# Order of the TensorE work in the dense expert loop: second table's product of block b-1 ahead of the first table's product of block b

## The chip, the core and the metric

One NeuronCore of a Trainium2 chip runs the whole program; the other seven cores are idle. The metric is device time of one execution in microseconds (us), lower is better; each time given is the median of several executions of the same compiled program. Engines are named as in the profile: PE is TensorE (matrix products), DVE is VectorE, ACT is ScalarE, POOL is GpSimd, SP is the engine that issues most plain DMA transfers.

## The reference

One step of a two-layer decoder on 576 tokens (512 of a prompt, 64 of samples). Each layer has a mixer and then an expert part, and the change lies in the expert part, which is run once per layer. It is this function (cut):

```
def peer_ffn(x, w_q, sub_keys, u, v):
    ...
    def block_fn(xb):
        q = (xb @ w_q).reshape(blk, PEER_HEADS, 2, PEER_HALF)
        s = jnp.einsum('thcd,hcnd->thcn', q, sub_keys).astype(jnp.float32)
        s_top, i_top = lax.top_k(s, PEER_TOPK)
        ...
        best_s, best_pos = lax.top_k(cand_s, PEER_TOPK)
        expert = jnp.take_along_axis(cand_e, best_pos, axis=-1)
        gate = jax.nn.softmax(best_s, axis=-1)
        act = jax.nn.gelu(jnp.einsum('td,thkd->thk', xb, u[expert]).astype(jnp.float32), approximate=False)
        return jnp.einsum('thk,thkd->td', (gate * act).astype(xb.dtype), v[expert])
```

There are 16384 experts per layer; expert e has a row u[e] and a row v[e] of 1024 floats (4 KB each). Every token picks 8 heads x 16 experts. Its result is the sum over the picked experts of gate x gelu(x . u[e]) x v[e].

## The kernel before

`peer_hybrid` (line 548) computes this sum in two ways side by side.

**Sparse part**: 256 prompt tokens and the 64 sample tokens get their rows by gather. There are 320 sets (`NSET`); for each set POOL issues one indirect DMA that fetches 128 rows of u into one of six slots `ug` (line 617), and, 20 sets later (`LAG`), one that fetches 128 rows of v into one of six slots `vg` (line 624). Each gather moves 512 KB. DVE does a dot product on each u set (`dot`, line 725) and adds each v set, weighted, to the accumulator (`add_row`, line 743). A slot is fetched again only when DVE is through with it. One pair of `dot` and `add_row` is a step; there are 340 steps.

**Dense part**: for the other 256 prompt tokens all experts are computed, in 128 blocks of 128 experts. For block b:

- SP loads 128 rows of each table, `du` (line 633) and `dv` (line 638), 512 KB each, each in two buffers.
- PE turns the u rows (`turn_rows`, line 839, into `pt`), and ACT copies them into `uT` (line 782).
- PE computes the first product, `hidden(b)` (line 863): rows of u times tokens, into one of two `hid` buffers; ACT applies gelu into one of two `gl` buffers (line 802).
- DVE multiplies by the gates (`product(b)`, line 713).
- PE computes the second product, `output(b)` (line 872): it adds the gated values times the v rows to `out`, which stays in PSUM for all 128 blocks.

In the trace every float32 matmul of the program stands as two records: `hidden` as 16, `output` as 8.

The two parts meet on DVE, whose order is written out: `product(b)`, then the two or three steps that `steps_of(b)` gives to block b (340 steps over 128 blocks: 84 blocks with three and 44 with two), then `product(b + 1)`.

PE's order is also written out. `hidden(b)` waits for the turned rows of b and for a free `hid` buffer; `output(b)` waits for `dv` of b and for `product(b)`:

```
                for b in range(NBLK):
                    if b + 1 < NBLK:
                        turn_rows(b + 1)
                    hidden(b)
                    if b:
                        output(b - 1)
                output(NBLK - 1)
```

SP's order in its turn b (line 669) is: in four turns after each quarter, a load of later gates, whose first waits for `product(b - 1)` (line 650); then `rows_u(b + 2)`, which waits until the rows of b are turned; then `rows_v(b + 1)`, which waits until `output(b - 1)` is done (line 637). So the loads of u stand in SP's queue behind a wait for `output`.

The layers' names begin with f (layer 0) and g (layer 1) in the trace: `fg_du`, `gg_du` and so on.

Of the kernel before, what the change touches and what calls it, by code (L numbers as in the profile page):

```python
# [531 lines left out]
def turn_batch(b):  # L532
    return TB0 + 2 * b + NGB * (b >= 1)
# [14 lines left out]
def peer_hybrid(nc, name, layer, hT, sel, idx, u_rows, v_rows, u_tab, v_tab, x_dram, g_dram, ident, iota128, u_in, v_in):  # L548
# [3 lines left out]
    with Phase(nc, name) as ph:  # L552
# [55 lines left out]
        with engines(nc) as block:  # L608
            @block.gpsimd
            def _(pool):  # L610
                for n in range(NSET + LAG):
                    if n < NSET:
                        if n >= NSLOT:
                            pool.wait_ge(dot_done, n - NSLOT + 1)
                        if n == first[PACK]:
                            pool.wait_ge(pair_in, 32)
                        pool.indirect_dma_start(  # L617
                            out=ug[:, n % NSLOT, :], out_offset=None, in_=u_rows,
                            in_offset=bass.IndirectOffsetOnAxis(ap=index(n), axis=0)).then_inc(u_in[n % NSLOT], 16)
                    if n >= LAG:  # L620
                        m = n - LAG
                        if m >= NSLOT:
                            pool.wait_ge(v_done, m - NSLOT + 1)
                        pool.indirect_dma_start(  # L624
                            out=vg[:, m % NSLOT, :], out_offset=None, in_=v_rows,
                            in_offset=bass.IndirectOffsetOnAxis(ap=index(m), axis=0)).then_inc(v_in[m % NSLOT], 16)
# [206 lines left out]
            @block.tensor  # L833
            def _(pe):
                def turn(n, m, srcs):
                    if n >= 2:
                        pe.wait_ge(ev_done, n - 1)
                    for k, src in enumerate(srcs):
                        last = pe.transpose(pt[0:m, n % 2, k, :], src, ident[:, :])  # L839
                    last.then_inc(tr_done, 1)  # L840

                def turn_rows(b):
                    pe.wait_ge(du_in[b % 2], 16 * (b // 2 + 1))
                    for c in range(2):
                        turn(turn_batch(b) + c, P, [du[:, b % 2, (4 * c + k) * P:(4 * c + k + 1) * P] for k in range(4)])

                def build():
                    for t in range(DTOK):
                        n = GATE0 + t // GB
                        if t % GB == 0:  # L850
                            pe.wait_ge(ev_done, n - 1)
                        pe.wait_ge(oh_made, t + 1)
                        last = pe.matmul(pt[:, n % 2, t % GB, :], ohj[:, t % OHR, :], ohi[:, t % OHR, :],
                                         start=True, stop=True)
                        if t % GB == GB - 1:
                            last.then_inc(oh_used, 1)

                def hidden(b):
                    pe.wait_ge(ev_done, turn_batch(b) + 2)
                    if b >= 2:  # L860
                        pe.wait_ge(gl_done, b - 1)
                    for k in range(KD):
                        last = pe.matmul(hid[:, b % 2, 0:DTOK], uT[:, b % 2, k, :], hT[:, k, DT0:DT0 + DTOK],  # L863
                                         start=(k == 0), stop=(k == KD - 1))
                    last.then_inc(hid_done, 1)

                def output(b):
                    pe.wait_ge(dv_in[b % 2], 16 * (b // 2 + 1))
                    pe.wait_ge(pr_done, b + 1)
                    for r in range(DTILES):  # L870
                        for c in range(2):
                            last = pe.matmul(out[:, r, 512 * c:512 * c + 512], gl[:, b % 2, r * P:(r + 1) * P],  # L872
                                             dv[:, b % 2, 512 * c:512 * c + 512], start=(b == 0), stop=(b == NBLK - 1))
                    last.then_inc(o_done, 1)

                for r in range(DTILES):
                    turn(r, P, [sel[:, GTILES + r, a, :, :].rearrange("p h k -> p (h k)") for a in range(3)])
                for r, i in enumerate(row_of):
                    t0, m = TILES[i]
                    for c in range(2):  # L880
                        turn(DTILES + 2 * r + c, m, [hT[:, 4 * c + k, t0:t0 + m] for k in range(4)])
                turn_rows(0)
                build()
                for b in range(NBLK):
                    if b + 1 < NBLK:
                        turn_rows(b + 1)
                    hidden(b)
                    if b:
                        output(b - 1)
                output(NBLK - 1)  # L890


# [2495 lines left out]
```

## Time and profile before

| what | value |
|---|---|
| median of 3 runs | 5568.41 us (5567.93 to 5584.46) |
| the profiled execution, its own time | 5593.84 us |
| span of its trace | 5592.0 us |
| busy: PE, DVE, POOL, ACT | 81%, 57%, 36%, 18% of the span |
| HBM read, written | 1062.95 MB, 46.08 MB |
| dense loop of layer 0 | from about 1381 us to 2582 us of the span |
| dense loop of layer 1 | from about 4362 us to 5562 us |

The profile is of one execution. A stretch is given as start and end in us from the span's start. The granted clock is the share of TensorE's full clock (2.4 GHz) that it got: 1.00 is 2.4 GHz, 0.50 is 1.2 GHz. The DMA share is the mean busy share of the core's 16 DMA engines.

### The profile page before, as it was taken

How to read it: one execution, taken by the hardware profiler on the slowest of the kernel's cores; microseconds unless marked ns; L12 is line 12 of the kernel's file. 1: busy time of each engine (PE TensorE's matmuls, PEld its weight loads, DVE VectorE, ACT ScalarE, POOL GpSimd, SP SyncE). 2: the span in 40 equal slices, each digit the busy share in tenths (PEclk: the TensorE clock that was granted, in tenths of full speed). 3: DMA queues.
4: the chain of work that ended last, by engine and by line, in shares of the span. 5: the costliest groups of instructions: out<-in, count | busy, mean ns of one | idle time of the engine just before them, and what ended most of it. 6: DMA issues, size and time to landing. Idle time of an engine off the chain costs nothing. (4 is left out here: it accounts for less than half of the span.)

```text
span 5592.0 us, 55069 instructions
## 1 busy us (share of the span) xinstructions
PE 4516.8 (81%) x19814; PEld 3265.5 (58%) x19814; DVE 3163.1 (57%) x6991; ACT 985.4 (18%) x1970; POOL 2010.1 (36%) x1580
## 2 busy tenths in 40 slices
PE   7988678928988888886886999785846988888887
PEld 5476456716655555554564888754634655555554
DVE  1324531798676777775128333234498666777775
ACT  0112310115111111111113222100104211111111
POOL 0000310120666666661004333131021466666663
PEclk9975779969999999998897888657878999999998
DMA  2320122103999999995110000102203799999998
GB/s 86 87 67 1 32 81 83 50 18 115 383 409 409 409 409 409 409 408 192 41 57 8 1 1 1 35 8 68 88 9 93 289 406 409 409 409 409 409 409 319
DMA packets 426495, 1109.48 MB, mean 198 GB/s; under 512 B 71628, under 2 KB 178861, under 8 KB 425766
## 3 DMA queue, kind: packets, MB, share of 16 engines
q0 software_dynamic: 184320, 671.17, 30.3%
q1 hardware_dynamic: 241910, 434.85, 22.1%
q8 instruction: 157, 2.57, 0.2%
q14 instruction: 108, 0.88, 0.0%
HBM read 1062.95 MB, written 46.08 MB: 198 GB/s over the span
## 5 line engine op out<-in xcount | busy, mean ns | idle before, releaser
L617 POOL DMA_INDIRECT gg_ug<-in_peer_u,g_idx x320 | 405.3, 1266 | 381.0 <-DVE gg_act_in L725 311.3
L617 POOL DMA_INDIRECT fg_ug<-in_peer_u,f_idx x320 | 388.6, 1214 | 362.8 <-DVE fg_act_in L725 296.3
L863 PE MATMUL gg_hid<-g_hT,gg_uT 128*128 128x256 f32 x2048 | 494.2, 397 | 0.0
L863 PE MATMUL fg_hid<-f_hT,fg_uT 128*128 128x256 f32 x2048 | 487.4, 393 | 0.0
L743 DVE SCALAR_TENSOR_TENSOR fg_xacc<-fg_vg,fg_wgt,fg_xacc 128x1024 f32<-128x1024 f32 x320 | 411.7, 1286 | 127.7 <-DMA fg_vg<-in_peer_v,f_idx 118.2
L872 PE MATMUL fg_out<-fg_dv,fg_gl 128*128 128x512 f32 x1024 | 465.7, 598 | 16.2 <-DVE fg_gl L713 16.0
L743 DVE SCALAR_TENSOR_TENSOR gg_xacc<-gg_vg,gg_wgt,gg_xacc 128x1024 f32<-128x1024 f32 x320 | 411.6, 1286 | 102.6 <-DMA gg_vg<-in_peer_v,g_idx 93.5
L872 PE MATMUL gg_out<-gg_dv,gg_gl 128*128 128x512 f32 x1024 | 462.2, 594 | 7.0 <-DVE gg_gl L713 6.9
L725 DVE CUSTOM_DVE_ANT_0 fg_ug<-fg_ug,fg_px 128x1024 f32<-128x1024 f32 x320 | 391.4, 1226 | 104.2 <-DMA fg_ug<-in_peer_u,f_idx 103.0
L624 POOL DMA_INDIRECT fg_vg<-in_peer_v,f_idx x320 | 372.5, 1164 | 197.7 <-DVE fg_xacc L743 127.6
L863 PEld LDWEIGHTS gg_hid<-g_hT,gg_uT 128*128 128x128 f32 x2048 | 402.9, 202 | 55.7 <-issue 0.5
L725 DVE CUSTOM_DVE_ANT_0 gg_ug<-gg_ug,gg_px 128x1024 f32<-128x1024 f32 x320 | 391.1, 1225 | 75.9 <-DMA gg_ug<-in_peer_u,g_idx 75.0
L863 PEld LDWEIGHTS fg_hid<-f_hT,fg_uT 128*128 128x128 f32 x2048 | 397.4, 199 | 53.8 <-issue 0.5
L624 POOL DMA_INDIRECT gg_vg<-in_peer_v,g_idx x320 | 356.7, 1115 | 176.5 <-DVE gg_xacc L743 94.9
L872 PEld LDWEIGHTS fg_out<-fg_dv,fg_gl 128*128 128x128 f32 x1024 | 195.0, 192 | 214.2 <-issue 208.3
L872 PEld LDWEIGHTS gg_out<-gg_dv,gg_gl 128*128 128x128 f32 x1024 | 194.8, 191 | 200.4 <-issue 194.1
L839 PE MATMUL gg_pt<-top_cm,gg_du 128*128 128x128 f32 x1024 | 148.8, 292 | 138.9 <-DMA gg_du<-in_peer_u 137.5
L839 PEld LDWEIGHTS gg_pt<-top_cm,gg_du 128*128 128x128 f32 x1024 | 121.2, 148 | 230.7 <-DMA gg_du<-in_peer_u 211.9
L839 PE MATMUL fg_pt<-top_cm,fg_du 128*128 128x128 f32 x1024 | 146.0, 288 | 135.1 <-DMA fg_du<-in_peer_u 133.9
L839 PEld LDWEIGHTS fg_pt<-top_cm,fg_du 128*128 128x128 f32 x1024 | 119.1, 147 | 227.3 <-DMA fg_du<-in_peer_u 208.6
L782 ACT ACTIVATE gg_uT<-gg_pt 128x512 f32<-128x512 f32 x256 | 140.9, 595 | 593.2 <-PE gg_pt L839 593.0
L782 ACT ACTIVATE fg_uT<-fg_pt 128x512 f32<-128x512 f32 x256 | 140.3, 595 | 596.2 <-PE fg_pt L839 596.2
(593 smaller groups left out, 7489.1 us busy)
## 6 DMA issues: line engine op xcount, KB each, us to landing
fg_du<-in_peer_u SPq DMA_DIRECT2D x128, 512.0 KB, 9.0
fg_dv<-in_peer_v SPq DMA_DIRECT2D x128, 512.0 KB, 6.8
gg_du<-in_peer_u SPq DMA_DIRECT2D x128, 512.0 KB, 9.0
gg_dv<-in_peer_v SPq DMA_DIRECT2D x128, 512.0 KB, 6.8
awg_wt<-in_mix_w_out SPq DMA_DIRECT2D x4, 2048.0 KB, 7.6
fs_wt<-in_peer_w_q SPq DMA_DIRECT2D x8, 1024.0 KB, 5.7
scratch_gates<-fg_late SPq DMA_DIRECT2D x32, 256.0 KB, 2.6
fg_gates<-scratch_gates SPq DMA_DIRECT2D x16, 512.0 KB, 9.0
```

The source lines that it names most:

```text
L617: pool.indirect_dma_start(out=ug[:, n % NSLOT, :], out_offset=None, in_=u_rows, in_offset=bass.IndirectOffsetOnAxis(ap=index(n), axis=0)). ...
L624: pool.indirect_dma_start(out=vg[:, m % NSLOT, :], out_offset=None, in_=v_rows, in_offset=bass.IndirectOffsetOnAxis(ap=index(m), axis=0)). ...
L725: dve.tensor_tensor_reduce(out=ug[:, g % NSLOT, :], in0=ug[:, g % NSLOT, :], in1=px[:, row_of[i], :], scale=1.0, scalar=0.0, op0=ALU.mult, ...
L743: dve.scalar_tensor_tensor(xacc[:, r, :], vg[:, g % NSLOT, :], wgt[:, s % 2, k:k + 1], xacc[:, r, :], ALU.mult, ALU.add).then_inc(v_done, 1)
L782: act.activation(uT[:, b % 2, 4 * c:4 * c + 4, :], pt[:, n % 2, :, :], ACT.Copy).then_inc(ev_done, 1)
L839: last = pe.transpose(pt[0:m, n % 2, k, :], src, ident[:, :])
L863: last = pe.matmul(hid[:, b % 2, 0:DTOK], uT[:, b % 2, k, :], hT[:, k, DT0:DT0 + DTOK], start=(k == 0), stop=(k == KD - 1))
L872: last = pe.matmul(out[:, r, 512 * c:512 * c + 512], gl[:, b % 2, r * P:(r + 1) * P], dv[:, b % 2, 512 * c:512 * c + 512], start=(b == 0), ...
```

## The change

In PE's loop `output(b - 1)` is taken ahead of `hidden(b)`. Nothing else is edited; the instructions of DVE, ACT, POOL and SP and their order are the same.

```
                 for b in range(NBLK):
                     if b + 1 < NBLK:
                         turn_rows(b + 1)
-                    hidden(b)
                     if b:
                         output(b - 1)
+                    hidden(b)
                 output(NBLK - 1)
```

PE at the start of the dense loop of layer 0, before (`fg_pt` holds turned rows, `fg_hid` is written by `hidden`, `fg_out` by `output`; line 853 builds the gates ahead of the loop):

```order
L853 MATMUL fg_pt<-fg_ohi,fg_ohj 128x128 x256
L839 MATMUL fg_pt<-top_cm,fg_du 128x128 x8
L863 MATMUL fg_hid<-f_hT,fg_uT 128x256 x8
L839 MATMUL fg_pt<-top_cm,fg_du 128x128 x8
L863 MATMUL fg_hid<-f_hT,fg_uT 128x256 x8
L872 MATMUL fg_out<-fg_dv,fg_gl 128x512 x4
```

PE at the same place now:

```order
L853 MATMUL fg_pt<-fg_ohi,fg_ohj 128x128 x256
L839 MATMUL fg_pt<-top_cm,fg_du 128x128 x8
L863 MATMUL fg_hid<-f_hT,fg_uT 128x256 x8
L839 MATMUL fg_pt<-top_cm,fg_du 128x128 x8
L872 MATMUL fg_out<-fg_dv,fg_gl 128x512 x4
L863 MATMUL fg_hid<-f_hT,fg_uT 128x256 x8
```

The last two rows have changed places: `output(0)` now stands between the turning of block 2 and `hidden(1)`. The same holds in each of the 127 further turns.

PE at the end of the loop of layer 0, before:

```order
L839 MATMUL fg_pt<-top_cm,fg_du 128x128 x8
L863 MATMUL fg_hid<-f_hT,fg_uT 128x256 x8
L872 MATMUL fg_out<-fg_dv,fg_gl 128x512 x4
L863 MATMUL fg_hid<-f_hT,fg_uT 128x256 x8
L872 MATMUL fg_out<-fg_dv,fg_gl 128x512 x8
```

PE at the same place now:

```order
L839 MATMUL fg_pt<-top_cm,fg_du 128x128 x8
L872 MATMUL fg_out<-fg_dv,fg_gl 128x512 x4
L863 MATMUL fg_hid<-f_hT,fg_uT 128x256 x8
L872 MATMUL fg_out<-fg_dv,fg_gl 128x512 x4
L863 MATMUL fg_hid<-f_hT,fg_uT 128x256 x8
L872 MATMUL fg_out<-fg_dv,fg_gl 128x512 x4
```

Before, the two last `output` stood together behind `hidden(127)`; now `hidden(127)` stands between them.

## Rows read from the trace of the kernel before

**Rows 1.** The page: span, and GB/s moved in 40 equal slices of it
```profile
span 5592.0 us, 55069 instructions
...
GB/s 86 87 67 1 32 81 83 50 18 115 383 409 409 409 409 409 409 408 192 41 57 8 1 1 1 35 8 68 88 9 93 289 406 409 409 409 409 409 409 319
```

**Rows 2.** Stretches: busy us (instructions) PE, PEld, DVE, ACT, POOL; clock, DMA share, GB/s
```profile
1380.00:1440.00 60.00, 57.90 (x245) 40.72 (x243) 25.34 (x47) 14.00 (x28) 25.60 (x22) 1.00 0.75 283
1440.00:2510.00 1070.00, 926.70 (x3601) 622.92 (x3600) 767.35 (x1015) 169.44 (x356) 702.25 (x593) 0.96 1.03 409
2510.00:2582.00 72.00, 66.13 (x243) 42.51 (x242) 42.60 (x49) 9.68 (x21) 27.46 (x21) 0.95 0.81 301
...
4430.00:5480.00 1050.00, 912.16 (x3514) 617.45 (x3515) 747.27 (x994) 165.67 (x348) 688.04 (x580) 0.96 1.03 409
```

**Rows 3.** Waits, 1440 to 2510 us (layer 0): total us, times, longest
```profile
PE fg_pt L839 <- DMA fg_du<-in_peer_u: 130.3, 76, 5.0
...
DVE fg_gl L713 <- ACT fg_gl L802: 76.4, 31, 6.8
...
PE fg_out L872 <- DVE fg_gl L713: 12.6, 10, 2.9
```

**Rows 4.** Waits, 4430 to 5480 us (layer 1), same columns
```profile
DVE gg_gl L713 <- ACT gg_gl L802: 135.1, 47, 9.1
```

**Rows 5.** DMA issues, 1440 to 2510 us: count, KB each, median us to landing
```profile
fg_dv<-in_peer_v SPq DMA_DIRECT2D x113, 512.0 KB, 6.8
fg_du<-in_peer_u SPq DMA_DIRECT2D x113, 512.0 KB, 9.0
...
fg_ug<-in_peer_u,f_idx POOLq DMA_INDIRECT x296, 19.2
```

**Rows 6.** Timeline, one turn near the loop's start: start us, duration us, instruction, [idle before]
```profile
1394.34 3.62 PE L863 MATMUL fg_hid<-f_hT,fg_uT 128*128 128x256 f32 x16
...
1397.80 3.60 PE L872 MATMUL fg_out<-fg_dv,fg_gl 128*128 128x512 f32 x8
1398.00 0.38 ACT L802 ACTIVATE fg_gl<-fg_hid 128x256 f32<-128x256 f32 x1 [2.81 <-PE fg_hid L863]
1398.41 0.42 DVE L713 TENSOR_TENSOR fg_gl<-fg_gl,fg_gates 128x256 f32<-128x256 f32 x1 [3.90 <-ACT fg_gl L802]
...
1401.23 1.04 PE L839 MATMUL fg_pt<-top_cm,fg_du 128*128 128x128 f32 x8
...
1402.10 3.62 PE L863 MATMUL fg_hid<-f_hT,fg_uT 128*128 128x256 f32 x16
```

**Rows 7.** Timeline, a late product and the output behind it, near 2515 us
```profile
2515.21 0.41 DVE L713 TENSOR_TENSOR fg_gl<-fg_gl,fg_gates 128x256 f32<-128x256 f32 x1
...
2515.78 6.43 PE L872 MATMUL fg_out<-fg_dv,fg_gl 128*128 128x512 f32 x8 [3.41 <-DVE fg_gl L713]
```

**Rows 8.** The page, groups on DVE: mean ns of one behind the busy time
```profile
L743 DVE SCALAR_TENSOR_TENSOR fg_xacc<-fg_vg,fg_wgt,fg_xacc 128x1024 f32<-128x1024 f32 x320 | 411.7, 1286 | 127.7 <-DMA fg_vg<-in_peer_v,f_idx 118.2
...
L725 DVE CUSTOM_DVE_ANT_0 fg_ug<-fg_ug,fg_px 128x1024 f32<-128x1024 f32 x320 | 391.4, 1226 | 104.2 <-DMA fg_ug<-in_peer_u,f_idx 103.0
```

**Rows 9.** Timeline, layer 0, DVE: products of blocks 1 and 8
```profile
1390.65 0.42 DVE L713 TENSOR_TENSOR fg_gl<-fg_gl,fg_gates 128x256 f32<-128x256 f32 x1 [2.23 <-ACT fg_gl L802]
...
1446.00 0.42 DVE L713 TENSOR_TENSOR fg_gl<-fg_gl,fg_gates 128x256 f32<-128x256 f32 x1 [2.50 <-ACT fg_gl L802]
```

**Rows 10.** Timeline, layer 0: product of block 120; outputs of blocks 126 and 127
```profile
2521.55 0.42 DVE L713 TENSOR_TENSOR fg_gl<-fg_gl,fg_gates 128x256 f32<-128x256 f32 x1
...
2574.72 7.03 PE L872 MATMUL fg_out<-fg_dv,fg_gl 128*128 128x512 f32 x16
```

**Rows 11.** Timeline, layer 1: product of block 120; outputs of blocks 126 and 127
```profile
5503.50 0.42 DVE L713 TENSOR_TENSOR gg_gl<-gg_gl,gg_gates 128x256 f32<-128x256 f32 x1
...
5554.34 7.03 PE L872 MATMUL gg_out<-gg_dv,gg_gl 128*128 128x512 f32 x16
```

**Rows 12.** Stretch with the late output (columns of rows 2)
```profile
2510.00:2520.00 10.00, 6.59 (x16) 3.59 (x16) 7.66 (x11) 0.38 (x1) 4.24 (x4) 0.73 0.99 385
```

More of the change, by code:

```diff
@@ L886, in _ @@
                         turn_rows(b + 1)
-                    hidden(b)
                     if b:
                         output(b - 1)
+                    hidden(b)
                 output(NBLK - 1)
```

## The prediction

> **What bounds the kernel now.** I read the page's slices first, then the loop's stretches, then the waits inside a stretch, and last the timeline of single turns. The slices [rows 1] show two plateaus at 409 GB/s, slices 11 to 17 and 33 to 39: the dense loops of the two layers, in which gathers and table loads run together. The stretches [rows 2] divide the first loop into three. From 1380 to 1440 us (the start) PE is busy 57.90 of 60 us and DMA moves 283 GB/s; from 1440 to 2510 us (the middle) DMA moves 409 GB/s with a busy share of 1.03, while PE is busy 87% and DVE 72%; from 2510 to 2582 us (the end) PE is busy 66.13 of 72 us and DMA falls to 301 GB/s. The middle of layer 1, 4430 to 5480 us, again shows 409 and 1.03. So **the DMA engines bound the two middles, 2120 us together, and PE bounds two starts and two ends of some 60 to 80 us each**. In the middle the waits say the same: PE waits 130.3 us for u rows, and only 12.6 us for DVE's products [rows 3].
>
> A block in the middle takes 1070/113 = 9.47 us, by the 113 loads of each table [rows 5]. PE needs less: in a turn with no wait, `hidden` takes 1397.80 - 1394.34 = 3.46 us, `output` 1401.23 - 1397.80 = 3.43 and the turning 1402.10 - 1401.23 = 0.87, together 7.76 us [rows 6].
>
> **The change part by part.** No instruction is added or removed, so bytes, DVE work and PE work stay; only when things start can change. Before, `hidden(b)` filled the time in which ACT and DVE made the gated values of block b-1. Now PE has the turning of one block there and nothing else.
>
> *The new chain.* `output(b)` -> `hidden(b+1)` -> gelu -> `product(b+1)` -> `output(b+1)` is now a closed ring. From the end of `hidden` to the gelu's start is 1398.00 - 1397.80 = 0.20 us, the gelu takes 0.38, the product starts 0.03 after it and takes 0.42 [rows 6]; from the end of a product to the `output` that waits for it is 2515.78 - (2515.21 + 0.41) = 0.16 [rows 7]. That is 1.19 us, and the ring is 3.43 + 3.46 + 1.19 = **8.08 us, against 7.76 before**: the turning (0.87) hides in the 1.19, and 0.32 us of PE idleness per block is left. This counts only where PE sets the pace.
>
> *What moves earlier.* `output(b-1)` ends 3.46 us sooner in its turn, and with it SP's release for the v rows of b+1 and the u rows queued behind them. Between that issue and the turning of those u rows there was one turn, 9.47 us, for a landing of 9.0 us [rows 5]; now there are 9.47 + 3.46 = 12.9 us. Most of the 130.3 us that PE waits for u rows should go. I cost that at no gain in the middle: PE's wait was covered by DMA, whose rate stays. What is late next is the product, for which PE will wait instead.
>
> *What moves later.* `hidden(b)` and so `product(b)` come 3.43 us later in the turn. DVE waits for a product with its two or three steps queued behind it, and POOL's next gathers wait for these steps. A step costs 1.226 + 1.286 = 2.51 us [rows 8], so DVE needs 7.96 us for a block of three steps and 5.44 for one of two; with the ring at 8.08 a block takes some 8.1 us when DMA is prompt, 1.4 us less than DMA allows. In a block of two steps, for which DMA takes 7.7 us (four gathers and two table loads of 0.524 MB, 3.15 MB at 409 GB/s; with three steps 4.19 MB, 10.3 us), the ring can hold DVE back by about 0.4 us. The cover is the depth of the gather queue: a gather lands 19.2 us after its issue [rows 5], and at 593 gathers on POOL in 1070 us [rows 2] that is 0.554 x 19.2 = 10.6 in flight of twelve slots, 5.6 MB or 13 us of DMA work. The best evidence is layer 1: there DVE already waits 135.1 us for gelu, up to 9.1 us at once [rows 4], and DMA stays at 409. I take **0 us for both middles**; if the cover were gone, each of 44 short blocks would cost up to 8.08 - 5.44 = 2.6 us.
>
> *The two starts.* In layer 0 product 1 now comes behind an `output`, 3.43 us later, and product 8 seven rings of 8.08 later: 1390.65 + 3.43 + 56.56 = 1450.6 instead of 1446.0 [rows 9], 4.6 us late. `output(7)` comes about 2.3 us early (3.45 early at block 0, less 7 x 8.08 minus the 55.35 us that blocks 1 to 8 took). A block brings 2.66 gathers of u, 1.39 MB, and 1.05 MB of table rows per 7.9 us. So at the moment DMA fills up, 4.6 x 0.176 = 0.81 MB of gathers are late and 2.3 x 0.133 = 0.31 MB of table rows early; 0.50 MB at 409 GB/s is **1.2 us**. Bounds: 0, and all 4.6. Layer 1 runs the same start; the same 1.2.
>
> *The two ends.* Dots are over at block 120, and from there PE sets the pace. With product 120 where it was, `output(127)` starts seven rings and 0.58 us later: layer 0, 2521.55 + 56.56 + 0.58 = 2578.7 against 2574.72 + 3.43 = 2578.15 [rows 10], **+0.5 us**; layer 1, 5503.50 + 57.14 = 5560.6 against 5554.34 + 3.43 = 5557.8 [rows 11], **+2.9 us**. Layer 0 loses less since a slow stretch lay there: its `output` at 2515.78 took 6.43 us [rows 7]. Bounds: 0, and 7 x 0.32 plus two uncovered 1.19 = 4.6 per layer.
>
> *The sum.* 1.2 + 1.2 + 0.5 + 2.9 = +5.8 us, bounds 0 and 18.4. A gain is excluded in starts and ends because their rings only grow. On the profiled execution that is 5592.0 + 5.8 = 5597.8 of span, 1.84 more for its own time. The median of the runs is 25.4 us (0.45%) under that execution's 5593.84; with the same distance the forecast is 5568.4 + 5.8 = **5574 us**.
>
> **The rivals.**
>
> *A, slower: a late clock.* PE's idleness now lies ahead of each `output` instead of ahead of the turning. After a wait of 3.41 us the `output` at 2515.78 took 6.43 us instead of 3.60 [rows 7], and the stretch shows a granted clock of 0.73 [rows 12], so part of it at 1.2 GHz. In the middles the clock is 0.96, some 8% of the time at 1.2 GHz [rows 2]. If a drop follows the wait in each block, costing half of those 2.83 us, the ring is 8.08 + 1.42 = 9.5 us; all of them, 10.9 us. It decides from a mean ring of 9.47 us on. Midway, 10.2 us, it adds 0.7 x 2120/9.47 = 157 us: 5731; just past the point it adds a few tens. Against it: once the ring sets the pace, PE has only 0.32 us of idleness left per block, and drops have stood behind waits of microseconds; the loss feeds on waits that it ends. The Trainium skill, TensorE: Matmul & The Clock Gate, section HAM oscillation — how this bites in real kernels, says that a loop which waits between bursts of matmuls starts each burst at the half clock; by that rule each block pays and the time would be nearer 5731. The 0.96 of rows 2 agrees in part: waits of u rows already come in two blocks of three, and most of the time stays at 2.4 GHz.
>
> *B, faster: the load latency was the bound.* Table loads, turning, `output` and SP's queue formed a loop of their own, with 9.0 us of landing per turn, close to 9.47. If that loop set the pace and DMA only looked full, DVE's waits for gelu, 76.4 + 135.1 us [rows 3, 4], would shrink, and up to 211 us with them: 5357. Against it: 409 GB/s does not move in either middle, whichever engine waits. The Trainium skill, DMA: Bandwidth & Descriptors, section Where 436 GB/s comes from, puts the ceiling at 435 GB/s; by that figure an estimated 2120 x (1 - 409/435) = 127 us could be saved, but the flat 409 at a share of 1.03 is nearer to a ceiling of its own.
>
> *C, slower: SP's wait for gates.* At blocks 16, 32, 48 and 64 SP waits for `product(b-1)` ahead of the next u rows. That product now follows `output(b-2)`, SP's previous release, by 3.46 + 0.20 + 0.38 + 0.03 + 0.42 = 4.5 us instead of coming at about the same time. The u rows then land some 9.9 us after the product (0.9 of issue, 9.0), while the ring wants them turned at 8.08 + 0.16 less 0.87: about 2.5 us late, eight times, 20 us in all if nothing covers it: 5594. Against it: the same 13 us of queued gathers.
>
> **How the numbers follow.** Forecast 0.76, A 0.14, B 0.05, C 0.05. About 0.3%, 17 us, is what a measurement of this kernel can tell from no change. The forecast's own bounds, 5568 to 5587, lie nearly all inside that; A and a little of the forecast and C give slower, B faster: 0.05 faster, 0.75 same, 0.20 slower. The range takes the forecast's bounds, 6 us below for the scatter of the runs, and C above: 5562 to 5595, with A and B left out.
>
> **What would show it.** Right: 409 GB/s unchanged in both middles; PE's wait for u rows down from 130 to under 40 us per layer and its wait ahead of `output` up from 12.6 to about 100; products near the loop's start 8.1 us apart; the first `output` near 1386.6 instead of 1390.0 us; SP waiting some 4 to 5 us at line 650 four times per layer. Wrong: slices of the middle below 400 GB/s, with POOL waiting longer for DVE and DVE for gelu (A, C, told apart by the clock and by the distance between such dips), or above 410 (B).

## The result and the profile after

| | before | after |
|---|---|---|
| median of 11 runs each | 5580.77 us (5566.6 to 5599.02) | 5604.76 us (5580.62 to 5612.77) |
| ratio, 95% interval | | 1.004, 1.0023 to 1.0057 |
| profiled execution, its span | 5593.84 us, 5592.0 us | 5606.07 us, 5604.2 us |

The change makes the kernel slower by 0.4%. The forecast was 5574 us, 0.1% above the 5568.41 us known then, in a range that ends at 5595; the measured time lies above it. Some 12 us of the miss are the base: eleven runs of the kernel before have their median at 5580.77 us, the three shown ahead at 5568.41. The rest is the change itself: 13 to 32 us by the interval where 6 were forecast.

The stretches after, each loop cut at 80 us and 1110 us behind its first product and at the first final addition (line 769, where DVE adds `out` to its rows); columns as in [rows 2]:

```profile
1383.02:1463.02 80.00, 78.63 (x316) 53.21 (x315) 40.61 (x69) 14.39 (x30) 40.84 (x35) 1.00 0.86 315
1463.02:2493.02 1030.00, 901.10 (x3429) 595.08 (x3428) 743.55 (x978) 158.54 (x339) 703.80 (x570) 0.96 1.03 409
2493.02:2588.09 95.07, 85.39 (x323) 55.50 (x321) 54.63 (x63) 14.06 (x30) 38.80 (x30) 0.96 0.79 300
4370.58:4450.58 80.00, 78.63 (x316) 53.20 (x316) 40.55 (x69) 14.39 (x30) 40.75 (x35) 1.00 0.85 316
4450.58:5480.58 1030.00, 889.21 (x3424) 590.64 (x3423) 743.56 (x978) 158.39 (x339) 694.09 (x571) 0.96 1.03 409
5480.58:5571.25 90.67, 84.26 (x327) 55.60 (x325) 54.12 (x63) 14.06 (x30) 38.98 (x30) 1.00 0.83 313
```

Both middles stay at 409 GB/s with a share of 1.03 and a clock of 0.96, exactly as in [rows 2]. The same cuts in one more execution of the kernel before (experiment 11), without its middles:

```profile
1389.34:1469.34 80.00, 77.17 (x318) 53.25 (x319) 43.20 (x73) 14.80 (x31) 42.74 (x37) 1.00 0.86 329
2499.34:2583.02 83.68, 77.02 (x296) 49.75 (x294) 51.38 (x58) 12.68 (x27) 35.24 (x28) 1.00 0.88 333
4361.97:4441.97 80.00, 77.77 (x320) 53.31 (x318) 43.95 (x73) 14.80 (x31) 43.33 (x37) 1.00 0.87 333
5471.97:5556.20 84.23, 76.39 (x291) 50.30 (x289) 52.21 (x59) 12.47 (x26) 36.17 (x28) 0.98 0.85 323
```

What DMA missed of 409 GB/s in a stretch is its length x (1 - rate/409). Starts: 15.6 and 14.9 us before, 18.4 and 18.2 after. Ends: 15.6 and 17.7 before, 25.3 and 21.3 after. The same bytes are moved, so this shortfall is the loss: 3 us at each start and 4 to 10 at each end. In the middle no loss shows, where 1 GB/s would be 2.5 us. In the profiled execution of the kernel before, cut in the same way, the ends miss 19.2 and 16.4 us; against that one the ends lose 6 and 5 us.

The waits of layer 0 from 1440 to 2510 us answer to [rows 3]:

```profile
PE fg_out L872 <- DVE fg_gl L713: 113.5, 98, 5.4
...
DVE fg_gl L713 <- ACT fg_gl L802: 82.6, 56, 4.9
...
PE fg_pt L839 <- DMA fg_du<-in_peer_u: 16.3, 9, 3.5
```

PE's wait for u rows fell from 130.3 to 16.3 us, and its wait for products rose from 12.6 to 113.5. DVE waits for gelu about as long as before (76.4). In layer 1, from 4430 to 5480 us, that wait fell from 135.1 us [rows 4]:

```profile
DVE gg_gl L713 <- ACT gg_gl L802: 76.5, 50, 4.3
```

SP's own waits in layer 0, 1440 to 2510 us:

```profile
SPq L650 <- DVE fg_gl L713: 17.1, 4, 5.1
```

### The profile page after: what moved, and what is told of

Read it like the earlier page. It is cut to its first block and busy times, and to the rows that moved or that the text cites. A ratio compares the mean times of both kernels' runs of the same rounds, so it can differ in the third digit from the quotient of the medians.

```text
span 5604.2 us, 55069 instructions
## 1 busy us (share of the span) xinstructions
PE 4532.8 (81%) x19814; PEld 3251.5 (58%) x19814; DVE 3172.9 (57%) x6991; ACT 980.0 (17%) x1970; POOL 2055.6 (37%) x1580
## 5 line engine op out<-in xcount | busy, mean ns | idle before, releaser
L872 PE MATMUL fg_out<-fg_dv,fg_gl 128*128 128x512 f32 x1024 | 514.2, 649 | 123.4 <-DVE fg_gl L713 121.9
L872 PE MATMUL gg_out<-gg_dv,gg_gl 128*128 128x512 f32 x1024 | 502.6, 637 | 135.6 <-DVE gg_gl L713 133.5
L863 PE MATMUL gg_hid<-g_hT,gg_uT 128*128 128x256 f32 x2048 | 462.9, 379 | 0.0
L624 POOL DMA_INDIRECT gg_vg<-in_peer_v,g_idx x320 | 383.9, 1200 | 195.1 <-DVE gg_xacc L743 118.8
L1689 POOL TENSOR_TENSOR ass_lar<-a_cb,ass_la 128x512 f32<-128x512 f32 (+1 forms) x20 | 27.1, 1367 | 595.7 <-DVE ass_cm L1751 592.0
L2631 POOL TENSOR_TENSOR rch_Lo<-rch_La,r_cb 128x512 f32<-128x512 f32 x96 | 121.4, 1278 | 309.5 <-PE rch_pg L2503 231.7
L802 ACT ACTIVATE gg_gl<-gg_hid 128x256 f32<-128x256 f32 x128 | 49.1, 384 | 990.4 <-PE gg_hid L863 990.4
L802 ACT ACTIVATE fg_gl<-fg_hid 128x256 f32<-128x256 f32 x128 | 49.1, 384 | 990.0 <-PE fg_hid L863 990.0
L416 POOL TENSOR_TENSOR fs_hit<-fs_hit,fs_itopf 128x1280 f32<-128x1280 f32 x16 | 55.4, 3483 | 433.6 <-DVE fs_hit L504 433.6
L2709 DVE TENSOR_TENSOR rch_XT<-rch_XT,rch_pg 128x512 f32<-128x512 f32 x96 | 66.1, 688 | 228.5 <-PE rch_pg L2513 227.6
```

The source lines that it names most:

```text
L416: pool.tensor_tensor(hit[:, a, :, :, :], hit[:, a, :, :, :], bc(itopf[:, h % 2, :, a, None, :], [P, n, TOPK, TOPK]), ALU.mult).then_inc(lo ...
L624: pool.indirect_dma_start(out=vg[:, m % NSLOT, :], out_offset=None, in_=v_rows, in_offset=bass.IndirectOffsetOnAxis(ap=index(m), axis=0)). ...
L802: act.activation(gl[:, b % 2, :], hid[:, b % 2, 0:DTOK], ACT.Gelu).then_inc(gl_done, 1)
L1689: pool.tensor_tensor(lar[0:m, q % 2, :, 0:m], bc(masks(i)[0][0:m, None, 0:m], [m, 4, m]), bc(la[0:m, i, 4 * q:4 * q + 4, None], [m, 4, m]) ...
L2631: pool.tensor_tensor(Lo[:, s, :, :], La[:, s, :, :], bc(lev[:, l + 1:l + 2, :], [P, 4, P]), ALU.mult).then_inc(lo_done[s], 1)
L2709: dve.tensor_tensor(XT[:, a, :, :], XT[:, a, :, :], pg[:, s, 1, :, :], ALU.add).then_inc(xt_done[s], 1)
```

## The experiments

The loop is followed by three parts, read from the starts of rows of line 713 and line 769: the **start** (product 0 to product 8), the **middle** (product 8 to product 120) and the **end** (product 120 to the first final addition). Layer 0 / layer 1, in us; the fifth column is the sum over both loops. Each row's parts are those of one execution. What lies outside the loops takes from 3170 to 3202 us in these executions, whatever PE's order in the loop; so the parts tell more than one execution's time does. The ratios are to the kernel before, timed beside each kernel.

| kernel | start | middle | end | both loops | ratio to before, 95% interval |
|---|---|---|---|---|---|
| before | 60.3 / 60.5 | 1075.6 / 1076.6 | 60.3 / 58.0 | 2391.2 | |
| 11: before again | 60.5 / 59.5 | 1075.3 / 1075.5 | 57.9 / 59.2 | 2387.9 | one execution |
| the change | 65.2 / 65.3 | 1078.4 / 1074.0 | 61.4 / 61.4 | 2405.7 | 1.004, 1.0023 to 1.0057 |
| 12: the change again | 65.3 / 65.2 | 1076.7 / 1074.0 | 61.4 / 61.4 | 2404.0 | one execution |
| 1: new order in turns 12 to 115 | 59.6 / 60.2 | 1075.5 / 1075.6 | 58.5 / 58.0 | 2387.3 | 1.0008, 0.9996 to 1.0021 |
| 2: in turns 1 to 11 | 65.3 / 65.5 | 1073.3 / 1072.9 | 58.9 / 58.4 | 2394.3 | 1.0008, 0.9993 to 1.0023 |
| 3: in turns 116 to 127 | 59.6 / 59.7 | 1079.8 / 1076.1 | 61.4 / 61.6 | 2398.3 | 1.0015, 1.0001 to 1.0029 |
| 10: as 3, table rows held back | 61.5 / 60.8 | 1073.7 / 1077.5 | 62.5 / 62.4 | 2398.5 | one execution |
| 4: full edges, old order | 66.3 / 68.2 | 1051.1 / 1042.6 | 63.7 / 66.6 | 2358.4 | 0.994, 0.9925 to 0.9955 |
| 8: full edges, new order | 65.3 / 66.3 | 1045.5 / 1046.9 | 66.9 / 65.5 | 2356.3 | 0.9937, 0.9924 to 0.9951 |
| 9: full edges, new order in 12 to 115 | 68.3 / 66.6 | 1042.3 / 1044.2 | 65.9 / 65.9 | 2353.2 | 0.992, 0.9906 to 0.9933 |
| 6: three slots, old order | 59.6 / 61.2 | 1087.1 / 1081.6 | 59.2 / 60.3 | 2408.9 | 1.0012, 0.9996 to 1.0028 |
| 7: three slots, new order | 65.6 / 66.4 | 1138.4 / 1109.7 | 61.4 / 61.9 | 2503.4 | 1.0167, 1.015 to 1.0185 |

**Experiments 1 to 3: one part of the loop alone.** Each takes the new order for some turns:

```
-                    hidden(b)
-                    if b:
+                    ahead = 12 <= b < 116
+                    if b and ahead:
+                        output(b - 1)
+                    hidden(b)
+                    if b and not ahead:
                         output(b - 1)
```

with `b < 12` in experiment 2 and `b >= 116` in experiment 3.

Experiment 1: 

> The output of block b-1 goes ahead of the first product of b in turns 12 to 115 alone; the 11 turns at the start and the 12 at the end of each loop keep the old order. Theory 'start and end' (the cost of the change lies where PE sets the pace, the middle is covered by the queued gathers): the start (product 0 to product 8) takes 60 us per layer as before, the end (product 120 to the first final addition) 58 to 60 us, the middle (product 8 to product 120) 1076 us within 3 us, and the time is that of the kernel before, ratio 0.999 to 1.001. Rival 'middle' (held back steps and half clock cost something in each block): the middle is 4 to 10 us longer per layer, ratio 1.0015 to 1.0035.

It fell out as "start and end" has it: 2387.3 us in both loops, as little as any kernel with the old order, although PE waits 113.8 us for products in layer 0's middle, as under the change. The rival "middle" falls by the parts, whose middles are no longer than before. The timed interval alone, which reaches 1.0021, would leave room for the rival's lower edge of 1.0015.

Experiment 2: 

> The new order in turns 1 to 11 alone. Theory 'start and end': product 8 comes 65 us after product 0 instead of 60, and none of the 5 us is made up before product 120, so each layer loses 5 us: +10 us, ratio 1.0018. Rival 'absorbed' (the prediction as written: the early table rows are credited when DMA fills up): product 8 is as late, but the middle is 3 to 4 us shorter, +2.4 us in all, ratio 1.0004. Rival 'middle': the start costs nothing in the end, ratio 1.000.

Here the first theory missed and the prediction's "absorbed" came nearest. Product 8 is 5 us late, but the middle is some 2 to 4 us shorter than with the old start; both loops are 3 to 6 us longer than in the two executions of the kernel before. The timed interval holds all three theories, so this rests on the trace. The products that show it (layer 0: 0, 8 and 120):

```profile
1392.54 0.43 DVE L713 TENSOR_TENSOR fg_gl<-fg_gl,fg_gates 128x256 f32<-128x256 f32 x1 [6.45 <-ACT fg_gl L802]
...
1457.85 0.43 DVE L713 TENSOR_TENSOR fg_gl<-fg_gl,fg_gates 128x256 f32<-128x256 f32 x1 [2.88 <-ACT fg_gl L802]
...
2531.18 0.42 DVE L713 TENSOR_TENSOR fg_gl<-fg_gl,fg_gates 128x256 f32<-128x256 f32 x1
```

From 1457.85 to 2531.18 are 1073.3 us, against 2521.55 - 1446.00 = 1075.6 before [rows 9, 10].

Experiment 3: 

> The new order in turns 116 to 127 alone. Theory 'start and end': start 60 us and middle 1076 us as before, the end 61.4 us in both layers instead of 60.3 and 58.0, so +1 and +3.4 us: +4.5 us, ratio 1.0008, in step with blocks 8.15 us apart. Rival 'middle': the end costs nothing that can be seen, ratio 1.000.

The end behind product 120 takes 61.4 and 61.6 us as expected, but the stretch ahead of it is longer too, by 4 us in layer 0. So both loops together lose 7 to 10 us where 4.5 were expected, the larger part of the change's cost. Where these 4 us lie is seen in the change itself, at products 119 and 120 of layer 0:

```profile
2516.39 0.42 DVE L713 TENSOR_TENSOR fg_gl<-fg_gl,fg_gates 128x256 f32<-128x256 f32 x1
...
2516.95 5.83 PE L872 MATMUL fg_out<-fg_dv,fg_gl 128*128 128x512 f32 x8 [4.63 <-DVE fg_gl L713]
...
2522.62 3.62 PE L863 MATMUL fg_hid<-f_hT,fg_uT 128*128 128x256 f32 x16
...
2526.69 0.42 DVE L713 TENSOR_TENSOR fg_gl<-fg_gl,fg_gates 128x256 f32<-128x256 f32 x1 [4.20 <-ACT fg_gl L802]
```

Product 119 is late in both kernels: 12.64 us behind product 118 here, 11.98 before, where it starts at 2515.21 [rows 7]. Before, `hidden(120)` was long done by then, and product 120 followed 6.34 us later, as soon as DVE had done its steps [rows 7, 10]. Now `hidden(120)` stands behind `output(119)`, which waits 4.63 us for the product and then takes 5.83 instead of 3.67 us; the granted clock is 0.72 from 2510 to 2520 us, so part of it ran at 1.2 GHz. Product 120 comes 10.30 us after product 119, with DVE idle for 4.20. The stretch recurs: in experiments 3 and 12 `output(119)` of layer 0 waits 4.64 and 4.63 us and takes 5.96 and 5.37, and product 120 comes 10.43 and 9.84 us after product 119. In layer 1 of the same three executions it comes 8.14 to 8.15 us after.

**Experiment 10: are table rows that run ahead paid back at the end?** As experiment 3, with one more wait in `rows_v`:

```
                     if b >= 2:
                         sp.wait_ge(o_done, b - 1)
+                    if b >= 117:
+                        sp.wait_ge(hid_done, b)
```

> As e3 (new order in turns 116 to 127 alone), but SP also waits for the first product of block b-1 before it loads the v rows of b, for b from 117, so that table rows are again asked for at the end of a turn as in the old order. Theory 'lead is paid back at the end' (with the new order table rows run half a block ahead of the products, DMA time that was spent early on them brings product 120 later): product 8 to product 120 takes 1075 to 1076.5 us again instead of 1080 and 1076 in e3, and product 120 to the first final addition 61.4 us, up to 1.5 more where PE then waits for u rows. Rival 'chance': product 8 to 120 stays near 1078.

Inconclusive. The mean middle, 1075.6, is what the theory asked for, but its two layers (1073.7 and 1077.5) scatter more than the difference sought, and the loops together lose as much as in experiment 3.

**Experiments 11 and 12: the scatter.** The kernel before and the change, unaltered.

> The kernel before once more, for the scatter of the loop's parts between executions: start 59.5 to 60.6 us, middle 1075 to 1077, end 58 to 60.5 in each layer, both loops together 2387 to 2393 us; what lies outside the loops between 3185 and 3202 us.

> The changed kernel once more. Theory 'start and end': start 65.2 to 65.4 us, middle 1074 to 1079, end 61.4 in each layer, both loops together 2403 to 2409 us, 12 to 18 us over the old order. Rival 'the middle pays in some executions': middle above 1082 us in a layer.

Both fell inside what was expected, but for one end of 57.9 us in experiment 11. The two executions of each order differ by 3.3 and 1.7 us over both loops, the two orders by 15.3 us between their means.

**Experiments 6 and 7: half the cover.** `NSLOT = 3` instead of 6, with either order.

Experiment 6: 

> Old PE order, three slots for each gathered table instead of six, so at most six gathers (3.1 MB, 7.7 us of DMA work at 409 GB/s) can be in flight instead of the 10.6 of twelve seen before. Both theories: DMA is no longer full in the middle, 330 to 400 GB/s, and the kernel is slower than before, ratio 1.01 to 1.10. It is the reference for the next run.

Experiment 7: 

> New PE order with three slots. Theory 'covered by queued gathers': with half the cover gone the hold-back of DVE behind the ring of 8.1 us shows in the middle, which becomes longer than with the old order and three slots by 0.2 to 1 us per block, 20 to 110 us per layer, ratio to the three slots of the old order 1.008 to 1.04. Rival 'the middle does not care about PE's order, whatever the cover': the two kernels with three slots differ by no more than the two with six do, up to 20 us.

The reference did not do what was expected: with the old order three slots per table can't be told from six by the times, 1.0012 (though the loops of its one trace are 19 us longer than the mean of the two with six). A gather then lands 8.8 us after its issue instead of 19.2, so half of the queue had only been waiting. But with the new order the cover is needed: 5681.71 against 5591.35 us, 1.6% more. The middles, from 1440 to 2500 and from 4430 to 5440 us, first with the old order, then with the new:

```profile
1440.00:2500.00 1060.00, 916.28 (x3518) 610.22 (x3517) 758.99 (x996) 165.17 (x347) 688.14 (x579) 0.96 1.02 405
4430.00:5440.00 1010.00, 865.60 (x3363) 577.63 (x3362) 725.81 (x953) 158.30 (x333) 657.53 (x556) 0.97 1.02 407
```

```profile
1440.00:2500.00 1060.00, 901.30 (x3341) 588.32 (x3340) 722.41 (x952) 154.09 (x330) 673.77 (x556) 0.92 1.00 387
4430.00:5440.00 1010.00, 868.82 (x3298) 573.29 (x3297) 696.28 (x925) 152.42 (x327) 658.79 (x534) 0.95 1.00 393
```

DMA falls to 387 and 393 GB/s, and the middles grow by 51 and 28 us, as the theory asked. In the new order's middle of layer 0 the waits are:

```profile
PE fg_out L872 <- DVE fg_gl L713: 146.4, 94, 6.9
...
DVE fg_gl L713 <- ACT fg_gl L802: 108.2, 55, 5.5
```

So PE does hold DVE back in the middle, and the queued gathers are what hides it. How much of the 51 and 28 us is the ring of 8.1 us and how much the clock is not separated. The clock falls as well, from 0.96 to 0.92 and from 0.97 to 0.95: in layer 0's middle 28 of 99 outputs take over 4 us, together 58 us more than 3.67 each, against 5 of 102 and 8.5 us with the old order.

**Experiments 4, 8 and 9: filling starts and ends.** DVE's steps are dealt out otherwise, four per block in the first and last five blocks:

```
+EDGE, FULL = 5, 4
 ...
 def steps_of(b):
-    total = NSET + LAG
-    return range(b * total // NBLK, (b + 1) * total // NBLK)
+    def upto(b):
+        rest = NSET + LAG - 2 * EDGE * FULL
+        mid = min(max(b - EDGE, 0), NBLK - 2 * EDGE)
+        return FULL * (min(b, EDGE) + max(b - NBLK + EDGE, 0)) + mid * rest // (NBLK - 2 * EDGE)
+    return range(upto(b), upto(b + 1))
```

Experiment 4, old order: 

> The old PE order, but DVE's steps are spread otherwise: four per block in the first five and the last five blocks of a loop (two or three before), 300 over the other 118. If starts and ends are stretches in which DMA runs at three quarters because PE sets the pace (theory 'start and end'), more gathers there fill it: four steps of one row and two table loads are 3.15 MB per turn of 7.76 us, 405 GB/s, and the middle then has 2.54 steps per block, 3.71 MB, 9.08 us at 409 GB/s. 118 x 9.08 + 10 x 7.8 = 1150 us per loop instead of 1196: up to 90 us less in all, ratio 0.984 to 0.990. If the loop's length were set otherwise, by DVE or by PE's own pace in the middle, the time would not move, ratio 0.998 to 1.002.

Experiment 8, new order throughout: 

> Steps spread as in e4 (four per block in the first five and last five blocks) with the new PE order throughout. Theory 'start and end': the ring of 8.15 us asks less of DMA at both edges, 7 us more per layer than e4, while the middle gives back the 3 to 4.5 us in which DMA was not full there, since PE no longer waits for u rows: +6 to +14 us against e4, ratio to the kernel before 0.995 to 0.9965. Rival 'full edges hide PE's order': equal to e4, 0.994 or less.

Experiment 9, new order in turns 12 to 115: 

> Steps spread as in e4, new PE order in turns 12 to 115 alone. Theory 'start and end': edges as in e4 (DMA not full for 6 to 7 and 6 to 9 us), the middle without PE's waits for u rows (128 us in e4) and DMA not full there for under 1 us instead of 3 to 4.5: 4 to 8 us less than e4 in all, ratio to the kernel before 0.9925 to 0.994. Rival: PE's waits for u rows cost nothing in e4 either, equal to e4 within 2 us.

All three beat the kernel before, by 0.6 to 0.8%, and so the change too. Their loops are 31 to 36 us shorter in all, a little over a third of the 90 us hoped for in experiment 4, which missed its 0.984 to 0.990. That figure left out a bound: a loop moves 475 MB, 1161 us at the 409 GB/s that no middle here exceeds, and the old loops, at about 1195 us, had only 34 us above it; 16 to 18 of these are won per loop. Layer 0 of experiment 9, cut as above:

```profile
1365.84:1445.84 80.00, 72.48 (x288) 49.16 (x287) 53.97 (x85) 13.44 (x28) 56.08 (x47) 0.98 0.96 376
1445.84:2475.84 1030.00, 918.54 (x3564) 612.23 (x3565) 733.26 (x971) 165.95 (x353) 689.72 (x562) 0.97 1.03 409
2475.84:2542.32 66.48, 57.88 (x213) 37.48 (x211) 48.45 (x55) 8.22 (x18) 30.30 (x27) 0.97 0.94 354
```

The start rose from about 330 to 376 GB/s. The last stretch, which begins 1110 us behind the first product, is 17 us shorter than in experiment 11 because the whole loop is. In experiment 4 the blocks of the middle have fewer steps, and PE became what DVE waits for there; the waits of its layer 0, 1440 to 2510 us:

```profile
DVE fg_gl L717 <- ACT fg_gl L806: 332.8, 111, 9.0
...
PE fg_pt L843 <- DMA fg_du<-in_peer_u: 127.6, 76, 5.6
```

(these rows carry the lines of that kernel: 717 and 806 are the product and the gelu, 843 the turning). In experiment 9 PE's wait for u rows is 27.5 us, and the loops are 5.2 us shorter than in experiment 4, within the 4 to 8 expected. The two timed intervals overlap. That the new order helps in the middle there is therefore seen in one trace each and not settled by the times. Experiment 8 missed: its theory asked for 0.995 to 0.9965, and the measured 0.9937 is what its rival "full edges hide PE's order" asked for. Its loops together are 2.1 us shorter than in experiment 4, less than two executions of the kernel before differ (3.3). So with the edges filled no cost of the new order is seen against the old one. Experiment 9, which keeps the old order at the edges, has loops 3.1 us shorter still, and timed intervals that overlap.

## Why the prediction was wrong, and where it was right

**Right: the bound and the middle.** Both middles stayed at 409 GB/s, PE's waits moved from u rows to products, and experiment 1 shows no cost of this. The reason given, the depth of the gather queue, is shown by experiment 7. The 0 us for the middles stands, and rival B falls with it: 114 us of PE's waits for u rows went in layer 0 and 59 us of DVE's waits for gelu in layer 1, and no time with them.

**Right: the ring.** Predicted 8.08 us, measured 1399.36 - 1391.21 = 8.15 us. One turn after the change (layer 0, `hidden(2)`):

```profile
1391.21 0.43 DVE L713 TENSOR_TENSOR fg_gl<-fg_gl,fg_gates 128x256 f32<-128x256 f32 x1 [5.47 <-ACT fg_gl L802]
...
1391.78 3.67 PE L872 MATMUL fg_out<-fg_dv,fg_gl 128*128 128x512 f32 x8 [0.15 <-DVE fg_gl L713]
...
1395.29 3.62 PE L863 MATMUL fg_hid<-f_hT,fg_uT 128*128 128x256 f32 x16
...
1399.36 0.42 DVE L713 TENSOR_TENSOR fg_gl<-fg_gl,fg_gates 128x256 f32<-128x256 f32 x1 [4.29 <-ACT fg_gl L802]
```

The difference is `output`: behind a wait it takes 1395.29 - 1391.78 = 3.51 us to the next `hidden`, not the 3.43 of [rows 6]. Product 8 was forecast 4.6 us late and is 5.

**Off: the base.** The forecast stood on a median of three runs, 5568.41 us. On the 5580.77 of eleven runs the same working gives 5586.6 us, and a range to some 5607, which would hold the measured time. So the base carries 12 of the 31 us of the miss, and the size of the change the other 18.

**Sized too low: the two starts.** Of the 4.6 us by which product 8 was to be late, the prediction charged only the late gathers, 0.81 MB or 2.0 us of DMA work, less 0.8 us for the early table rows: 1.2 per layer. Experiment 2 bears out that part of the lateness is made up, by middles 2 to 4 us shorter, but less of it: its loops lose 2.4 us per layer against the mean of the two executions of the old order. In the first 80 us after the change DMA moves 1.1 and 1.4 MB less than in experiment 11, where 0.50 MB were worked out. Which of the two terms was wrong is not shown.

**Wrong: "Dots are over at block 120, and from there PE sets the pace", and product 120 "where it was".** This is the step that failed. The ends were put at 0.5 and 2.9 us; experiment 3 shows 8.7 us for both loops, and the shortfall of DMA 4 to 10 us in each. Two things were left out. First, the old order does not keep PE's pace from block 120 on. With `hidden` done ahead, DVE takes some of the products 119 to 123 faster than PE's own 7.76 us and so makes up for a late one: 6.34 and 6.80 us from 119 to 121 in layer 0 before, and 6.47 and 3.56 from 121 to 123 in experiment 11:

```profile
2534.07 0.42 DVE L713 TENSOR_TENSOR fg_gl<-fg_gl,fg_gates 128x256 f32<-128x256 f32 x1
...
2540.54 0.42 DVE L713 TENSOR_TENSOR fg_gl<-fg_gl,fg_gates 128x256 f32<-128x256 f32 x1
...
2544.10 0.42 DVE L713 TENSOR_TENSOR fg_gl<-fg_gl,fg_gates 128x256 f32<-128x256 f32 x1 [0.57 <-ACT fg_gl L802]
```

The new order has no such stock and needs 8.15 for each. Second, in layer 0 a late product 119 is followed by a wait of 4.63 us and an `output` partly at 1.2 GHz: rival A's mechanism, at one block of layer 0 instead of at all of them. DMA moves 279 GB/s from 2520 to 2530 us there; that too few gathers were left to hide the wait is argued from this, not tested. Both are seen at once when the end is counted from product 119, which is late in each kernel: to the first final addition it takes 65.1 to 66.7 us in the two executions of the old order, and 71.2 to 71.8 in layer 0 and 69.6 to 69.8 in layer 1 with the new order there (the change, experiments 3 and 12). I had seen that stretch, [rows 7] and [rows 12], and took it as a reason for the change to lose less. The new order pays it in full.

**How it adds up.** Experiments 1, 2 and 3 against 2389.6 us, the mean of the two executions of the old order: -2.3, +4.8 and +8.7 us, together +11.2; the change as a whole +15.3 in its two executions. That is 0.27% and lies inside the timed interval, in its lower half; whether the few us up to its centre of 0.4% are more than chance is open. The kernel before, timed again beside the experiments, has medians of 5586.73 us (29 runs) and 5589.28 us (15 runs); the change's 5604.76 us lies 18 and 15 us above these, which speaks for the traces' figure, though these runs were not made beside the change's.

**The rivals.** A as a mean over the middle did not come: the clock stays at 0.96. PE's waits for u rows and products together hardly changed, 142.9 us before and 129.8 after, which may be why. By the rule of the Trainium skill (TensorE: Matmul & The Clock Gate, section HAM oscillation — how this bites in real kernels), each block would pay; the trace agrees at single waits, as at 2516.95, and not for the loop as a whole: 19 of 103 outputs in layer 0's middle took over 4 us, 1 of 105 before. C's waits came about as worked out, four per layer, 17.1 us in sum in layer 0 and 17.9 in layer 1, and cost nothing that shows in the middle. The bounds of the sum, 0 to 18.4 us, hold the 15.3 of the traces. The chance of 0.75 for "within 0.3%" took the lower half of these bounds for likely without a reason from a row.

## What to carry to other kernels

While enough transfers are queued to keep DMA full, it costs nothing that a pipeline stage (here PE) waits. A reordering that takes away the work which that stage had done ahead still costs time at the two ends of the loop, where the queue is not full. So cost a reordering by its start and its end, and read from the trace who sets the pace in the last blocks before and after, instead of holding one event in place. What DMA missed of its plateau rate, stretch by stretch, is the quickest account of such a loop. Here that account showed the edges as the only loss, and dealing the other stream's work out to them gained 0.6 to 0.8%, more than the new order of PE's work lost.

## What was not expected of the hardware

With the old order, six slots for gathers of 512 KB, beside the table loads, fill the DMA engines nearly as well as twelve: 405 to 407 GB/s against 409, with the time to landing falling from 19.2 to 8.8 us. Halving the slots changes the time by 0.1% with the old order (1.0012, 0.9996 to 1.0028) and by some 1.3% with the new one (1.0167 against 1.004, both to the kernel before).
